# Eight modulation tiles of every head unit on TensorE, four at a time on groups of 32 columns

## The reference

```python
cond = jax.nn.silu(c)
for layer in range(DEPTH):
    mod = cond @ w_ada[layer] + b_ada[layer]
    sh_m, sc_m, g_m, sh_f, sc_f, g_f = jnp.split(mod[:, None, :], N_MOD, axis=-1)
    h = rms_norm(x, norm_mix_gain[layer]) * (1.0 + sc_m) + sh_m
    ...
    x = x + g_m * y
    h = rms_norm(x, norm_ffn_gain[layer]) * (1.0 + sc_f) + sh_f
    x = x + g_f * swiglu(h, w_ffn_in[layer], w_ffn_out[layer])
return rms_norm(x, final_gain)
```

## Time and profile before

| | |
|---|---|
| Median of three runs | 2167.86 us (2167.64 to 2169.1) |
| The profiled execution: span, which is its own time here | 2165.9 us |
| First FFN product starts (L646) | 177.16 us |
| PE busy | 2130.7 us, 98% |
| DVE, ACT, POOL busy | 76%, 46%, 1% |
| DMA | 574.34 MB, 265 GB/s in the mean |
| TensorE's products of head tiles (L676) | 208 instructions, 57.2 + 42.3 us busy |

### The profile page before, as it was taken

The page is one execution under the profiler, slowest core; times in us unless marked ns, Lnnn a source line. Parts: engine busy times, 40 slices in busy tenths (PEclk is TensorE's granted clock), DMA queues, the critical chain, the costliest instruction groups (busy, mean ns, idle before and its releaser), DMA issues.

```text
span 2165.9 us, 24699 instructions
## 1 busy us (share of the span) xinstructions
PE 2130.7 (98%) x9533; PEld 1722.3 (80%) x9533; DVE 1640.7 (76%) x1693; ACT 998.1 (46%) x1117; POOL 22.4 (1%) x89
## 2 busy tenths in 40 slices
PE   7999999999999999999999999999999999999998
PEld 3557887888888888888888888878888888888886
DVE  5779998899988887779787887677755666456645
ACT  2324544444444434465555465544454444444344
POOL 1000000000000000020000000000000000000000
PEclk9999999999999999999999999999999999999999
DMA  9999997899999998756656654678855556568664
GB/s 383 419 418 348 359 331 267 298 321 337 319 354 330 342 340 289 254 200 237 210 198 216 222 196 163 193 276 296 284 185 188 186 181 193 186 193 295 239 214 146
DMA packets 149249, 574.34 MB, mean 265 GB/s; under 512 B 16678, under 2 KB 16870, under 8 KB 141452
## 3 DMA queue, kind: packets, MB, share of 16 engines
q1 hardware_dynamic: 149132, 572.77, 74.8%
HBM read 570.60 MB, written 2.10 MB: 264 GB/s over the span
## 4 chain that ended last, share of the span: by engine, by line
PE 93%; DVE 3%; DMA 2%; ACT 1%; issue 1%; SPq 0%; DVEq 0%; ACTq 0%
PE prod L646 28%; PE prod L650 28%; PE prod L647 28%; PE modp L676 2%; DVE acc L1396 2%; PE small L723 1%; DMA ada<-in_ada_sections 1%; PE small L908 1%; DMA ada_head<-in_ada_sections 1%; PE modp L683 1%; PE small L883 0%; PE modp L712 0%; DVE w_lo L1347 0%; PE prod L620 0%; PE prod L619 0%
## 5 line engine op out<-in xcount | busy, mean ns | idle before, releaser
L994 ACT ACTIVATE w_hi<-raw 128x1024 fp32r<-128x1024 f32 x696 | 736.3, 1061 | 975.9 <-PE prod L650 842.3
L1347 DVE TENSOR_TENSOR w_lo<-raw,w_hi 128x1024 fp32r<-128x1024 f32 x696 | 848.9, 1223 | 413.3 <-ACT w_hi L994 411.2
L646 PE MATMUL prod<-w_hi,h_hi 128*128 128x512 f32 x2072 | 817.2, 394 | 2.8 <-DVE part_gate L1746 1.1
L650 PE MATMUL prod<-w_hi,h_lo 128*128 128x512 f32 x2072 | 807.1, 390 | 0.0
L647 PE MATMUL prod<-w_lo,h_hi 128*128 128x512 f32 x2072 | 806.7, 389 | 0.0
L646 PEld LDWEIGHTS prod<-w_hi,h_hi 128*128 128x128 f32 x2072 | 389.1, 188 | 85.5 <-issue 2.9
L650 PEld LDWEIGHTS prod<-w_hi,h_lo 128*128 128x128 f32 x2072 | 388.9, 188 | 82.1 <-DVE h_lo L1505 0.3
L647 PEld LDWEIGHTS prod<-w_lo,h_hi 128*128 128x128 f32 x2072 | 389.3, 188 | 78.5 <-issue 1.0
L1396 DVE SCALAR_TENSOR_TENSOR acc<-ada,cond,acc 128x1024 f32<-128x1024 f32 x255 | 326.4, 1280 | 1.1 <-DMA ada<-in_ada_mixed 0.3
L646 PE MATMUL prod<-w_hi,g_hi 128*128 128x512 f32 x680 | 265.7, 391 | 0.0
L650 PE MATMUL prod<-w_hi,g_lo 128*128 128x512 f32 x680 | 264.6, 389 | 0.0
(11 more groups left out here) (207 smaller groups left out, 1082.5 us busy)
## 6 DMA issues: line engine op xcount, KB each, us to landing
raw<-in_w_ffn_in SPq DMA_DIRECT2D x352, 512.0 KB, 4.7
ada<-in_ada_sections SPq DMA_DIRECT2D x256, 512.0 KB, 6.1
raw<-in_w_ffn_out SPq DMA_DIRECT2D x176, 512.0 KB, 4.2
raw<-in_hgrn_w_in SPq DMA_DIRECT2D x128, 512.0 KB, 3.6
ada_head<-in_ada_sections SPq DMA_DIRECT2D x36, 1024.0 KB, 15.6
raw<-in_hgrn_w_out SPq DMA_DIRECT2D x32, 512.0 KB, 3.5
ada<-in_ada_sections SPq DMA_DIRECT2D x12, 1024.0 KB, 11.9
ada<-in_ada_mixed SPq DMA_DIRECT2D x16, 512.0 KB, 8.7
```

What stands on the lines that cost most here:

```text
L646: pe.matmul(o, hi[:, k, ts], wh, start=(begin and s == 0), stop=False)
L650: mm = pe.matmul(o, lo[:, k, ts], wh, start=False, stop=(end and s == n - 1))
L994: act.activation(w_hi[:, slot], raw[:, r], ACT.Copy).then_inc(hi_ready, 1)
L1347: dve.tensor_tensor(w_lo[:, slot], raw[:, r], w_hi[:, slot], ALU.subtract).then_inc(lo_ready, 1)
```

## The change

`PE_LOADS` becomes 8 for every head unit. `cond_rows` shrinks to 128 x 8 x 32: GpSimd clears it, and ScalarE copies the first eight columns of `cond` into column 0 of the eight blocks with one instruction. `multiply_loads` takes four tiles at a time. Tile 0 of four multiplies with 32 weight columns into rows 0 to 31 of `modp`, tile 1 into rows 32 to 63, and so on; the first halves of all four come first, then the second halves. Only rows 0, 32, 64 and 96 hold anything but zero. VectorE therefore adds all 128 rows of `modp` to its sum, in gate units too, and `reduce_unit` starts its product anew for them after waiting for that addition.

```diff
-    PE_LOADS = [7, 7, 7, 6, 8, 8, 9]
+    PE_LOADS = 8
+    GROUPS = 4
+    GROUP = P // GROUPS
...
-            cond_rows = sb("cond_rows", [P, max(PE_LOADS), P], where=pooling)
+            cond_rows = sb("cond_rows", [P, PE_LOADS, GROUP], where=pooling)
...
+            pool.memset(cond_rows[:, :, :], 0.0).then_inc(rows_begun, 1)
...
                 n_rows, _ = folded(u)
-                for k in range(n_rows):
-                    n = u * KD + k
-                    slot, _ = ada_slot(n)
-                    ada_arrived(pe, n)
+                for first in range(0, n_rows, GROUPS):
                     for o in range(2):
-                        mm = pe.matmul(modp[:, o], cond_rows[:, k], ada_buffer(slot)[:, o * CH:(o + 1) * CH], start=(k == 0),
-                                       stop=(in_columns(u) and k == n_rows - 1))
-                    mm.then_inc(ada_free[slot], 1)
+                        for k in range(first, first + GROUPS):
+                            n, part = u * KD + k, k - first
+                            slot, _ = ada_slot(n)
+                            if o == 0:
+                                ada_arrived(pe, n)
+                            mm = pe.matmul(modp[part * GROUP:(part + 1) * GROUP, o], cond_rows[:, k],
+                                           ada_buffer(slot)[:, o * CH:(o + 1) * CH],
+                                           start=(first == 0), stop=(first == n_rows - GROUPS))
+                            if o:
+                                mm.then_inc(ada_free[slot], 1)
...
-                a, begun = unit_buffer(u), u < len(HEAD)
-                if not begun:
-                    pe.wait_ge(unit_taken, u)
+                a = unit_buffer(u)
+                pe.wait_ge(unit_taken, u)
+                if u < len(HEAD):
+                    pe.wait_ge(row_added, u + 1)
                 for o in range(2):
-                    mm = pe.matmul(modp[:, o], ones[:, :], a[:, o * CH:(o + 1) * CH], start=not begun, stop=True)
+                    mm = pe.matmul(modp[:, o], ones[:, :], a[:, o * CH:(o + 1) * CH], start=True, stop=True)
...
-            for k in range(max(PE_LOADS)):
-                rows_k = act.activation(cond_rows[:, k], ones[:, :], ACT.Identity, bias=zero[:, 0:1], scale=cond[:, k:k + 1])
-            rows_k.then_inc(rows_ready, 1)
+            act.wait_ge(rows_begun, 1)
+            act.activation(cond_rows[:, :, 0], cond[:, 0:PE_LOADS], ACT.Copy).then_inc(rows_ready, 1)
...
-                if in_columns(u) and k == last - 1:
+                if u < len(HEAD) and k == last - 1:
                     ada_used(dve, n - 1)
                     ada_used(dve, u * KD + first - 1)
-                    row = a[0:1, :].rearrange("p (a n) -> p a n", a=2)
-                    dve.tensor_tensor(row, row, modp[0:1, :, :], ALU.add).then_inc(row_added, 1)
-                    dve.wait_ge(row_added, columns_before(u) + 1)
+                    both = a.rearrange("p (a n) -> p a n", a=2)
+                    dve.tensor_tensor(both, both, modp[:, :, :], ALU.add).then_inc(row_added, 1)
+                    dve.wait_ge(row_added, u + 1)
```

More of the change, by code:

```diff
@@ L152, in folded @@
             return 0, KD
-        return PE_LOADS[u], KD
+        return PE_LOADS, KD
     def in_columns(u):
@@ L291, in build @@
         pscale_loaded = sem("pscale_loaded")
+        rows_begun = sem("rows_begun")
         rows_ready = sem("rows_ready")
@@ L686, in head_columns @@
             def head_columns(u):
-                pe.wait_ge(row_added, columns_before(u) + 1)
+                pe.wait_ge(row_added, u + 1)
                 b = bias_column(u)
```

## The result

The changed kernel takes 2175.44 us (median of six runs, 2174.89 to 2176.02), the kernel before 2169.08 in its six runs beside them. The ratio is 1.003, with a 95% interval of 1.002 to 1.0041: slower by 0.3%, 6.4 us. The profiled executions have spans of 2173.2 and 2165.9 us. They lie 7.3 us apart and not 6.4, because the profiled execution of the kernel before is its fastest (2167.64 us), while the six spans of the changed kernel are 2173.0 to 2173.7. The kernel before has spans from 2165.7 to 2169.0 us in its executions, so that a difference of 1 us between two traces can be chance. The forecast was slower, 2172.5, with a range up to 2175.8.

What follows compares the result with a forecast made beforehand. The head ahead of the first FFN product was taken as the bound, VectorE from 155 us. Terms -0.4 + 1.4 + 1.6 + 2.4 = +5.0, less 0.4, gave +4.6 on 2167.86: 2172.5 us, range 2167.4 to 2175.8.

Steps and rivals of the forecast that it cites:

- What bounds the head: Ahead of the first FFN product: landings stand still, VectorE bounds from 155 us, and any delay moves the end equally.
- Unit 4: Bias ends at 123.0; TensorE idles some 6 us, its reduction runs at half clock, gate at 126.6, +1.2 us.
- Unit 5: TensorE's products are done by 148.5, or 151 at low clock; the reduction waits for VectorE until 151.6, -0.4 us.
- the sum does not change: TensorE's four-tile group, taken as 3.5 us: anything between 1.7 and 3.5 leaves the forecast total the same.
- sum of +5.0: Terms up to the FFN: -0.4 (unit 5), +1.4 (extra fold), +1.6 (column sum), +2.4 (winning the clock back).
- Unit 6: VectorE does one fold more, +1.39 us, and ends at 174.7; all tiles have landed, so no wait is added.
- The border's clock: Unit 6 to FFN: TensorE waits over 5 us, clock falls; column sum +1.6, regaining the clock +2.4 us, less 0.4.
- The clock holds: Rival, decided at 165 to 174 us: TensorE stays at 2.4 GHz; -0.3 to +1.0 us; chance 0.17.
- No overlap: Rival: column groups run one after another, eight tiles cost 13.9 us, unit 3 late; +3.5 to +7.5 us; chance 0.15.
- stay low through unit 5: Rival: narrow matmuls don't lift the clock, unit 5's reduction comes at 155.5; about +8 us, 2176; chance 0.08.
- its loss at the border was not short: Judges a rival: the clock falls but the tail wins it back at once; +1.5 to +4 us; chance 0.15.

Runs made afterwards that it cites:

- fill_full: Changed kernel plus unused TensorE products: eight and two ahead of units 4 and 5's reductions, four ahead of and eight behind unit 6's transposes; 2169.46 us, ratio 1.0001.
- best: Changed kernel with twelve unit 6 tiles on TensorE, normalisation ahead of VectorE's four folds, unused products ahead of both gate reductions and behind the transposes; 2166.51 us, ratio 0.9987.
- before_u6_8_fill: Kernel before with eight instead of nine unit 6 tiles on TensorE and four unused products behind the transposes; 2170.28 us, ratio 1.0006.
- twelve: Changed kernel with twelve unit 6 tiles on TensorE and the normalisation ahead of VectorE's four folds, no unused products; 2170.05 us, ratio 1.0004.
- fill_gates: Changed kernel with unused TensorE products ahead of the two gate reductions only, eight in unit 4 and two in unit 5; 2171.70 us, ratio 1.0014.
- small_add: Changed kernel, but in gate units 4 and 5 VectorE adds 2 x 2 columns of TensorE's sum instead of 2 x 512; 2171.71 us, ratio 1.0013.
- before_all8: Kernel before with eight tiles in every head unit on TensorE, 128 weight columns each, no column groups; 2176.76 us, ratio 1.0038.
- fill_all: Changed kernel with unused TensorE products ahead of both gate reductions and, four ahead of and six behind the transposes, in unit 6's waits; 2170.97 us, ratio 1.0009.
- fill_border: Changed kernel with ten unused TensorE products in unit 6's waits only, four ahead of the transposes and six behind; 2174.11 us, ratio 1.0022.

## Why the prediction was right, and where its sizes were off

The direction and the mechanism hold: slower, by VectorE's longer chain and by a clock that falls in the waits. The time lies inside the stated range. The forecast was +4.6 us over the kernel before, measured are +6.4 between the medians.

*What bounds the head.* Right: landings did not move (DMA share 1.02 and 1.01 in the same windows), and nothing behind the head gave a microsecond back. From the FFN's start to the end it is 1988.7 us before and 1988.8 to 1989.5 in the four experiments' kernels that kept or hardly lost the clock there (fill_full, best, before_u6_8_fill, twelve); where it stays low into the FFN, up to 1990.9.

*Unit 4.* Right, and nearly to the number: bias end 122.8 for 123.0, gate +1.24 for +1.2. Only the wait was longer, 8.30 us for "some 6", as pool product 1 was done at 114.6 us for 117.

*Unit 5.* This term was mis-sized. The forecast had the reduction start at 151.6 (151.83 measured) but priced it at full clock. It took 3.78 us instead of 1.88, and fill_gates and small_add show that this is the clock. The forecast's own numbers held a warning: products done by 148.5 and a reduction at 151.6 leave TensorE idle for 3.1 us, as long as the 3.00 us that it had named as what lost the clock at 30. It asked what this wait does to the clock in unit 4 and at the border, and not here. In small_add a wait of 2.20 us kept the clock in this place, here one of 4.25 lost it; a wait of 3.1 was not tried. A smaller error added to it. I took 3.5 us for a group of four tiles and wrote that between 1.7 and 3.5 "the sum does not change". The groups ran fully beside each other: in unit 2, at full clock, one group of 16 instructions follows the other after 1.74 us.

```profile
62.77 1.92 PE L683 MATMUL modp<-ada,cond_rows 128*32 128x512 f32 x16
64.51 1.90 PE L683 MATMUL modp<-ada_head,cond_rows 128*32 128x512 f32 x16
```

So pool products 2 and 3 were done by 147.6 instead of 148.5 and the wait was 4.25 us. The gate of unit 5, and with it VectorE's update, came 1.7 us later than before where -0.4 was forecast. These 2.1 us are what the sum of +5.0 lacks up to the +6.9 at the seventh FFN matmul, and the border came out 0.2 under its 4.0. The total of +4.6 took another 0.4 off, and lies 2.7 us under the +7.3 between the traces. That it is only 1.8 from the medians' +6.4 is luck in part.

*Unit 6.* Right: an extra fold costs 1.39 on VectorE (3.13 less the gate's 1.73 is 1.40), and 1.3 at the FFN in before_u6_8_fill.

*The border's clock.* Forecast 1.6 + 2.4 less 0.4, together 3.6. Measured 1.7 for the sum (4.8 less 3.1) and 2.1 for fillers and first products (6.9 less 4.8), 3.8. Right, though the stretch lasted longer than named: 164.9 to 185.2 us for "around 170 to 183".

*The rivals.* "The clock holds" did not happen, and fill_full shows that its price was right: held by force, the kernel is at 1.0001 of the kernel before, inside the -0.3 to +1.0 us. "No overlap" did not happen either, as a group took 1.74 us at full clock; before_all8, which computes its way but without the additions in the gate units, came out at +7.6 us between the medians, just above its +3.5 to +7.5. The clock was back at 1.00 from 127.4 to 151.1, so it did not stay low through unit 5, and its loss at the border was not short.

## What to carry to other kernels

Before you make hidden work on TensorE faster, look at what it will wait for afterwards and what stands behind that wait: the instruction behind a longer wait may be on the path and run at half clock. Here the freed time had to be filled, with work taken from the bound engine (four more tiles of unit 6) and with products of no use; either alone only broke even (1.0004 and 1.0001), both together gave 0.13% (0.9987, 0.9978 to 0.9996). When you size a term, size the idle time that it leaves on TensorE too, even where the term itself looks free.

## What the runs showed of the hardware

Matmuls with 32 weight columns into four different groups of 32 PSUM rows ran fully beside each other: 16 instructions of 128x512 f32 in 1.74 us at full clock, where 16 with 128 columns take 6.94. The Trainium skill (TensorE: Matmul & The Clock Gate, Part 3) reports 2.38x for three column tiles; here four gave 4.0x (6.94 over 1.74). The Trainium skill also names a drain when the tiling mode changes (TensorEngine Tiling (Array Packing), Tiling Modes); here it does not show as a cost: in unit 5 the pool product with 128 columns starts at 136.37 us, when the last group, twelve instructions from 134.53 that take 1.91, is just ending.

I had not expected so short a wait to matter: 1.75 us idle ahead of the row addition, then a few small matmuls and one-column matmuls, and the clock was low within the column sum in fill_all and fill_border, while 1.83 us between wide matmuls before 127.27 did not lose it. Two more fillers in those 1.75 us kept it (fill_full). What else the chip goes by these runs do not show. The same sixteen one-column matmuls took 1.84 to 1.95 us at full clock and 3.41 to 3.57 at half.
